# Sparse attention on one core: output projection in one stage, two groups' scores in the other bank ring, last query behind the scores

## What is computed

```python
proj = h @ w_in
q = rope_2(proj[..., :N_HEADS * HEAD_DIM] ...)
...
sc = einsum('bghqd,bgcd->bghqc', qb, kc) * scale        # compressed scores
p_c = masked_softmax(sc, ...);  o_c = p_c @ vc
p_s = masked_softmax(qb @ ks_g * scale, mask_s);  o_s = p_s @ vs_g
p_w = masked_softmax(qb @ kw * scale, mask_w);    o_w = p_w @ vw
out = gb[..., 0:1] * o_c + gb[..., 1:2] * o_s + gb[..., 2:3] * o_w
...
return o @ w_out
```

## Time and profile before

| | |
|---|---|
| runs of the kernel before | 1603.38, 1600.79, 1595.78 us; median 1600.79 |
| the profiled execution | 1603.51 us, of which the span of the trace is 1601.7 |
| TensorE busy | 1500.8 us, 94% of the span |
| VectorE, ScalarE busy | 1053.1 us (66%), 874.3 us (55%) |
| chain that ended last | 79% TensorE, 9% VectorE, 6% ScalarE, 3% transfers |
| mean granted clock of TensorE | 0.972 |

### The profile page before, as it was taken

How to read it: one execution, slowest core, us unless ns; L and a number is a source line. 1 busy time by engine, 2 the same in 40 slices (tenths; PEclk the granted TensorE clock), 3 DMA queues, 4 the chain that set the end, 5 groups by cost and what they waited for, 6 DMA issues and landing times.

```text
span 1601.7 us, 25719 instructions
## 1 busy us (share of the span) xinstructions
PE 1500.8 (94%) x10589; PEld 1410.6 (88%) x10589; DVE 1053.1 (66%) x1626; ACT 874.3 (55%) x1541; POOL 88.7 (6%) x141
## 2 busy tenths in 40 slices
PE   6998999999989989999999899999999888899997
PEld 6998889999989888899999799987998777899876
DVE  5645559886766366698868678855566434688744
ACT  6465557564554646564645666644566333566544
POOL 9100000006000000000000100000000000000000
PEclk9999999999999999999999999999899798999998
DMA  7524366566646143665666455565343011565561
GB/s 220 160 73 138 106 197 183 163 185 171 216 134 171 46 137 109 207 185 168 184 195 210 141 183 184 171 190 165 106 124 118 14 40 54 171 184 184 172 197 66
DMA packets 214692, 241.14 MB, mean 151 GB/s; under 512 B 19240, under 2 KB 185282, under 8 KB 214576
## 3 DMA queue, kind: packets, MB, share of 16 engines
q1 hardware_dynamic: 208672, 228.66, 47.8%
q0 software_dynamic: 5904, 10.85, 2.5%
HBM read 238.42 MB, written 1.05 MB: 150 GB/s over the span
## 4 chain that ended last, share of the span: by engine, by line
PE 79%; DVE 9%; ACT 6%; DMA 3%; issue 2%; POOL 0%; DVEq 0%; POOLq 0%
PE bank L589 23%; PE bank L593 22%; PE bank L592 22%; DVE w_lo L1642 2%; PE bank L688 2%; PE bank L760 2%; ACT w_hi L1160 2%; PE bank L1062 1%; DMA raw<-in_ffn_up 1%; ACT S L1328 1%; DMA raw<-in_w_in 1%; PE bank L1048 1%; PE bank L964 1%; DMA raw<-in_mla_w_ukv 1%; PE bank L788 1%
## 5 line engine op out<-in xcount | busy, mean ns | idle before, releaser
L1642 DVE TENSOR_TENSOR w_lo<-raw,w_hi 128x1024 fp32r<-128x1024 f32 (+2 forms) x460 | 523.8, 1154 | 296.2 <-ACT w_hi L1160 293.9
L589 PE MATMUL bank<-h_hi,w_hi 128*128 128x256 f32 (+1 forms) x2024 | 577.7, 285 | 21.1 <-DVE w_lo L1642 5.9
L1160 ACT CAST w_hi<-raw 128x1024 fp32r<-128x1024 f32 (+2 forms) x460 | 453.5, 991 | 244.7 <-DMA raw<-in_w_in 89.8
L592 PE MATMUL bank<-h_lo,w_hi 128*128 128x256 f32 (+1 forms) x2024 | 575.4, 284 | 0.0
L593 PE MATMUL bank<-h_hi,w_lo 128*128 128x256 f32 (+1 forms) x2024 | 575.3, 284 | 0.0
L589 PEld LDWEIGHTS bank<-h_hi,w_hi 128*128 128x128 f32 (+1 forms) x2024 | 390.1, 193 | 23.2 <-issue 17.9
L593 PEld LDWEIGHTS bank<-h_hi,w_lo 128*128 128x128 f32 (+1 forms) x2024 | 390.0, 193 | 0.0
L592 PEld LDWEIGHTS bank<-h_lo,w_hi 128*128 128x128 f32 (+1 forms) x2024 | 389.9, 193 | 0.1
L589 PE MATMUL bank<-w_hi,h_hi 128*128 128x512 f32 (+1 forms) x272 | 104.6, 384 | 12.9 <-DVEq L2386 10.2
L592 PE MATMUL bank<-w_lo,h_hi 128*128 128x512 f32 (+1 forms) x272 | 102.9, 378 | 0.0
L593 PE MATMUL bank<-w_hi,h_lo 128*128 128x512 f32 (+1 forms) x272 | 102.7, 378 | 0.0
(11 more groups left out here) (353 smaller groups left out, 2396.5 us busy)
## 6 DMA issues: line engine op xcount, KB each, us to landing
raw<-in_w_in SPq DMA_DIRECT2D x160, 512.0 KB, 3.8
raw<-in_ffn_up SPq DMA_DIRECT2D x88, 512.0 KB, 3.6
raw<-in_ffn_down SPq DMA_DIRECT2D x40, 512.0 KB, 4.4
raw<-in_w_proj_a SPq DMA_DIRECT2D x16, 512.0 KB, 3.4
raw<-in_w_proj_b SPq DMA_DIRECT2D x16, 512.0 KB, 3.4
raw<-in_w_out SPq DMA_DIRECT2D x16, 512.0 KB, 4.6
raw<-in_ple_gate SPq DMA_DIRECT2D x16, 512.0 KB, 3.8
raw<-in_w_proj_c SPq DMA_DIRECT2D x16, 384.0 KB, 3.3
```

The source lines that it names most:

```text
L589: first = pe.matmul(out_, lh, rh, start=start, stop=False)
L592: pe.matmul(out_, lh, rl, start=False, stop=False)
L1160: act.copy(w_hi[b][:, 0:size], raw[b][:, 0:size]).then_inc(sems["hi_done"], 1)
L1642: dve.tensor_tensor(w_lo[b][:, 0:size], raw[b][:, 0:size], w_hi[b][:, 0:size].bitcast(F32), ALU.subtract).then_inc(sems["w_split"], 1)
```

## The change

Four things, all of them a matter of order and of banks; the instructions and their sizes stay.

- The projection is one stage: project 0, C3, then projects 1, 2 and 3.
- With the J banks no longer held open, the scores of groups 2 and 3 and C1 take J banks (`LATE_SCORES`, thirteen J jobs, after which each engine advances J by 13). `score_job`, `scored`, `score_ring` choose the ring.
- Query 3 comes behind S1, and swap 3 behind X0. The new order of TensorE: S0, swap 2, S1, q3, X0, swap 3, V0, cs, S2, ct0, ct1, X1, V1, C0, S3, C1, X2, V2, X3, C2, V3, project 0, C3, project 1, 2, 3.
- ScalarE and VectorE follow: the splits of `w_out`'s first four pieces stand behind X0 on ScalarE and behind the three first operations on `Tc` on VectorE; ScalarE loads its exponential table with a small extra activation into `sink`; of X's banks VectorE copies 0, 1 and 4, ScalarE 2, 3 and 5.

```diff
@@ -181,12 +181,14 @@
 NSA_JOBS = (["bias"] + [f"norm{u}" for u in range(KT // 2)] + ["hidden", "keys0", "keys1", "kc", "vc", "gates", "kc_swap", "swap0", "swap1"]
-            + [f"S0.{i}" for i in range(6)] + ["swap2"] + [f"S1.{i}" for i in range(6)] + ["swap3", "cs"]
-            + [f"X0.{i}" for i in range(6)] + ["V0.1", "V0.0"] + [f"S2.{i}" for i in range(6)] + ["ct0", "ct1", "C0"]
-            + [f"X1.{i}" for i in range(6)] + ["V1.1", "V1.0"] + [f"S3.{i}" for i in range(6)] + ["C1"]
-            + [f"X2.{i}" for i in range(6)] + ["V2.1", "V2.0", "C2"]
-            + [f"X3.{i}" for i in range(6)] + ["V3.1", "V3.0", "C3"])
+            + [f"S0.{i}" for i in range(6)] + ["swap2"] + [f"S1.{i}" for i in range(6)]
+            + [f"X0.{i}" for i in range(6)] + ["swap3", "V0.1", "V0.0", "cs", "ct0", "ct1"]
+            + [f"X1.{i}" for i in range(6)] + ["V1.1", "V1.0", "C0"]
+            + [f"X2.{i}" for i in range(6)] + ["V2.1", "V2.0"] + [f"X3.{i}" for i in range(6)]
+            + ["C2", "V3.1", "V3.0", "C3"])
 NSA_AT = {name: n for n, name in enumerate(NSA_JOBS)}
+LATE_SCORES = {f"S{g}.{i}": 6 * (g - 2) + i for g in (2, 3) for i in range(6)}
+LATE_SCORES["C1"] = 12
 KV_ORDER = (0, 1, 2, 4, 3, 5)
@@ -952,8 +954,26 @@
 
+            def score_job(name):
+
+                if name not in LATE_SCORES:
+                    return job(name)
+                b = w.bank("J", LATE_SCORES[name])
+                pe.wait_ge(free[b], w.turn("J", LATE_SCORES[name]))
+                return b
+
+            def scored(name, mm, b):
+
+                mm.then_inc(sems[f"full{b}"], 1)
+                if name not in LATE_SCORES:
+                    w.go("K", 1)
+
             def emptied(name):
 
+                if name in LATE_SCORES:
+                    b = w.bank("J", LATE_SCORES[name])
+                    pe.wait_ge(free[b], w.turn("J", LATE_SCORES[name]) + 1)
+                    return
                 n = k0 + NSA_AT[name]
@@ -1016,19 +1036,20 @@
                 for n in range(4):
-                    b = job(f"S{g}.{n}")
+                    b = score_job(f"S{g}.{n}")
                     pe.matmul(ps[b][:, :], q2[:, 2 * g + n // 2, P:TOK],
                               kz[:, n % 2, g, :, :].rearrange("p a k -> p (a k)"), start=True, stop=False)
-                    filled(pe.matmul(ps[b][:, :].rearrange("p (a k) -> p a k", a=2)[:, :, P:TOK], ident_r[:, :],
-                                     causal_r[:, :].unsqueeze(1).to_broadcast([P, 2, P]), start=False, stop=True), b)
+                    scored(f"S{g}.{n}", pe.matmul(
+                        ps[b][:, :].rearrange("p (a k) -> p a k", a=2)[:, :, P:TOK], ident_r[:, :],
+                        causal_r[:, :].unsqueeze(1).to_broadcast([P, 2, P]), start=False, stop=True), b)
                 for u in range(2):
-                    b = job(f"S{g}.{4 + u}")
+                    b = score_job(f"S{g}.{4 + u}")
                     pe.matmul(ps[b][:, :].rearrange("p (a k) -> p a k", a=4), ident_r[:, :],
...
                                        q2[:, 2 * g + u, 0:P], kz[:, n, g, :, 0:P], start=False, stop=n == 1)
-                    filled(mm, b)
+                    scored(f"S{g}.{4 + u}", mm, b)
 
@@ -1064,7 +1085,7 @@
 
-                b = job(f"C{g}")
+                b = score_job(f"C{g}")
                 pe.wait_ge(sems["o_ready"], 2 * g + 2)
@@ -1072,19 +1093,18 @@
                                        om[:, g % 2, qt, u * P:(u + 1) * P], c["ident"], start=False, stop=qt == 1)
-                filled(mm, b)
+                scored(f"C{g}", mm, b)
 
...
 
-                if g == 0:
-                    for bank in range(4):
-                        pe.wait_ge(free[w.bank("J", bank)], w.turn("J", bank))
                 pe.wait_ge(sems["o_split"], g + 1)
...
                         bank = w.bank("J", u)
+                        if k == 0:
+                            pe.wait_ge(free[bank], w.turn("J", u))
                         cols = slice(n * 512, (n + 1) * 512)
@@ -1107,10 +1127,12 @@
             scores2(0)
-            query(3)
             swap(2)
             scores2(1)
+            query(3)
+            turn2(0)
             swap(3)
+            values2(0)
             b = job("cs")
@@ -1121,27 +1143,28 @@
             w.go("S", 4), w.go("J", 8)
-            turn2(0)
-            values2(0)
             scores2(2)
...
                                               for g in (2 * i, 2 * i + 1) for qt in range(TT)])
+            turn2(1)
+            values2(1)
             emptied("vc")
...
             combine2(0)
-            project2(0)
-            turn2(1)
-            values2(1)
             scores2(3)
             combine2(1)
-            project2(1)
-            for g in (2, 3):
-                turn2(g)
-                values2(g)
-                combine2(g)
+            turn2(2)
+            values2(2)
+            turn2(3)
+            combine2(2)
+            values2(3)
+            w.go("J", 13)
+            project2(0)
+            combine2(3)
+            for g in (1, 2, 3):
                 project2(g)
@@ -1570,15 +1593,20 @@
 
+            def score_ring(name):
+
+                return ("J", LATE_SCORES[name]) if name in LATE_SCORES else ("K", at(name))
+
             def query(i):
                 for n in range(2):
-                    hi(i, n)
+                    if i < 2:
+                        hi(i, n)
                     evac("J", 2 * i + n, q2[:, 2 * i + n, :], scale=SCALE2)
...
                 for i in range(6):
-                    b = w.bank("K", at(f"S{g}.{i}"))
+                    b = w.bank(*score_ring(f"S{g}.{i}"))
                     act.wait_ge(sems["t_max"], w.taken("t_max"))
@@ -1586,42 +1614,46 @@
                         ins_ = act.activation(dst, src, ACT.Exp, bias=nm[:, r, e:e + 1], accum_out=sums[:, r, e:e + 1])
-                    ins_.then_inc(free[w.bank("K", at(f"S{g}.{i}"))], 1)
+                    ins_.then_inc(free[b], 1)
 
             def turned2(g):
-                for n in (1, 3):
+                for n in (2, 3):
                     evac("K", at(f"X{g}.{n}"), t1T[:, n, :, :].rearrange("p b n -> p (b n)"), width=512)
...
             def high_o(g):
-                b = w.bank("K", at(f"C{g}"))
-                act.wait_ge(full[b], w.turn("K", at(f"C{g}")))
+                ring = score_ring(f"C{g}")
+                b = w.bank(*ring)
+                act.wait_ge(full[b], w.turn(*ring))
                 act.copy(h_hi[:, 2 * g:2 * g + 2, :].rearrange("p a n -> p (a n)"), ps[b][:, :])\
...
                 query(i)
+            act.activation(sink[:, :], c["eps"], ACT.Exp)
             exps2(0)
+            exps2(1)
             query(3)
-            exps2(1)
+            turned2(0)
+            for j in (2, 3):
+                hi(j, 0), hi(j, 1)
             act.wait_ge(sems["tc_ready"], 1)
...
             w.go("S", 4), w.go("J", 8)
-            turned2(0)
             exps2(2)
...
                 evac("K", at(f"ct{i}"), tcT[:, 2 * i:2 * i + 2, :].rearrange("p a n -> p (a n)"), width=512)
+            turned2(1)
             high_o(0)
-            turned2(1)
             exps2(3)
-            hi(0, 0), hi(0, 1)
             high_o(1)
             turned2(2)
-            hi(1, 0), hi(1, 1)
+            turned2(3)
             high_o(2)
-            turned2(3)
-            hi(2, 0), hi(2, 1)
+            w.go("J", 13)
+            hi(0, 0), hi(0, 1)
             high_o(3)
-            hi(3, 0), hi(3, 1)
+            for j in (1, 2, 3):
+                hi(j, 0), hi(j, 1)
             for u, (n, t) in enumerate(QUARTERS):
@@ -2328,12 +2360,17 @@
 
-            def maxima(g):
+            def score_ring(name):
+
+                return ("J", LATE_SCORES[name]) if name in LATE_SCORES else ("K", at(name))
+
+            def maxima(g, which=range(6)):
 
                 r = g % 2
-                for i in range(6):
-                    b = w.bank("K", at(f"S{g}.{i}"))
-                    dve.wait_ge(full[b], w.turn("K", at(f"S{g}.{i}")))
+                for i in which:
+                    ring = score_ring(f"S{g}.{i}")
+                    b = w.bank(*ring)
+                    dve.wait_ge(full[b], w.turn(*ring))
                     if i < 4:
@@ -2344,7 +2381,8 @@
                 for i in range(6):
-                    dve.wait_ge(free[w.bank("K", at(f"S{g}.{i}"))], w.turn("K", at(f"S{g}.{i}")) + 1)
+                    ring = score_ring(f"S{g}.{i}")
+                    dve.wait_ge(free[w.bank(*ring)], w.turn(*ring) + 1)
                 settle(dve.reciprocal(rg[:, r, :], sums[:, r, :]))
@@ -2352,7 +2390,7 @@
 
-                for n in (0, 2, 4):
+                for n in (0, 1, 4):
                     b = w.bank("K", at(f"X{g}.{n}"))
@@ -2376,13 +2414,14 @@
 
-                b = w.bank("K", at(f"C{g}"))
-                dve.wait_ge(full[b], w.turn("K", at(f"C{g}")))
+                ring = score_ring(f"C{g}")
+                b = w.bank(*ring)
```

(34 more changed lines are left out.)

## The result

The changed kernel took **1580.1 us** (median of 4 runs, 1577.4 to 1585.8) against 1599.9 for the kernel before (4 runs): ratio 0.988, 95% interval 0.985 to 0.991. The forecast was 1579, from 1570 to 1591. Over all of them the changed kernel's median is 1582.5 (30 runs, 1572.4 to 1592.6) and that of the kernel before 1596.9 (45 runs, 1587.2 to 1606.4). The gain over many runs is therefore 14.4 us, less than the 21.5 that the sum took off the profiled execution. Why is the subject of the next sections.

The account below looks back on a forecast made before the run. TensorE bounds the attention stretch by work, gaps and half-speed time: 1226.5 + 92.6 work + 9.9 gaps + 3 low clock + 1.9 idle puts ple at 1333.9, 21.5 us earlier; from the 1600.8 median, 1579 us (1570 to 1591).

Parts of the forecast that it names:

- the sum: Total of all terms: the ple product behind the projection starts at 1333.9 instead of 1355.4, 21.5 us earlier.
- First scores: End of S0: 1.2 us earlier, as a weight split leaves VectorE's queue before the second rotation; bounds 0 and 1.3.
- The way to cs: From S0's end to cs's end: work, with cs at 3.5 us and swaps at 1.0, plus 0.8 of bank waits in S1.
- The first gap: In S2: S2.4 waits 4.6 us for exponentials, delayed by VectorE's Tc operations and four weight splits, until 8.5 after cs.
- the clock step: Low clock behind the second gap, in X1 and V1, costs 3 us, bounds 0 and 7; behind the first, largely hidden.
- The second gap: In X1: X1.2 waits 4.0 us, until 17.0 after cs, for ScalarE to empty ct0's bank behind S2's exponentials.
- V1 to the end: From V1 on nothing waits long: no wait over 0.7 us to V3's end; the low_o and om waits go.
- The clock rival: Clock stays low from X1 to V3, 35 us of work taking twice as long: 1611 us, chance 0.07 for the full case.
- Transfers and late VectorE: Two rivals: projection paced by its transfers, 1585 to 1587, chance 0.1; VectorE late at nine steps, 1585, chance 0.1.
- The tail: After the projection TensorE idles 1.9 us, where it idled 0.4, before the ple product; behind that nothing differs.

Follow-up runs that it names:

- the second experiment: Changed kernel with ScalarE copying ct0, ct1 and its part of X1 after the first two of S2's six banks of exponentials: 1573.5 us against 1583.4.
- e10: The changed kernel with nothing altered, run a fourth time: 1580.9 us.
- e7: The changed kernel with nothing altered, run again on the chip of the second group of experiments: 1582.1 us.
- e1: Changed kernel with VectorE's four weight splits moved ahead of its wait for the compressed scores: 1576.9 us against 1583.4.
- e5: Changed kernel with the last query put back ahead of swap 2 and of S1's exponentials on ScalarE: 1580.4 us against 1582.1.
- e8: Changed kernel with LATE_SCORES emptied (one bank ring) and the last query back ahead of swap 2: 1581.0 us against 1580.9.

## Why the prediction was right, and where it was not

**First scores.** Forecast −1.2; swap 2 now starts 6.3 us after S0's start where the query did at 7.4: 1.1. Right.

**The way to cs.** Forecast 26.15 us from the end of S0 to the end of cs. TensorE starts S2 at 1254.01, 32.3 after S0's start at 1221.74, of which S0 is 6.3: 26.0. The bank waits in S1 that I put at 0.8 were 0.2 and a swap 0.9 for 1.0, but cs took 4.0 and not 3.5, half of its time at clock 0.50: three small misses that cancel.

**The first gap.** The place and the time of its end are right, its size is not. The sum had S2.4 start 8.5 us after cs; it started at 1262.62, 8.6 after. But TensorE waited there 1.6 us and not 4.6, because it ran the four banks before it at clock 0.51 (1253 to 1260 in the first view). So the term of the wait was 3.0 too high, and the same 3.0 went into low clock at no cost to the end. Filling a wait with half-speed work is what "largely hidden" in the clock step meant, but it named no clock that falls ahead of the gap: nothing waited there, and the clock fell inside cs in every trace of the changed kernel.

**The second gap.** Forecast: S2.5 free at 10.6 after cs, `tc_done` at 11.1, X1.2 at 17.0, a wait of 4.0. Measured: ct runs from 1265.05 (11.0), X1.2 at 1270.89 (16.9), wait 3.9. Right, and for the reason given, as the second experiment showed by moving only ScalarE's order.

**The clock: the term that was mis-sized.** Forecast 3 us behind the second gap, bounds 0 and 7. In the first trace X1's rest took 3.5 for 1.8, V1 10.1 for 5.4 and C0 3.2 for 1.9: 7.7 us, just over the upper bound. The rows I had (a low stretch of 9 us) gave no such length, and no single row could have: four traces of one kernel gave 17 us of it twice (7.7 and 7.6 us lost), once about 3 us (1.5 lost, e10) and once none behind that wait (e7). The mean loss is 4.2. That the forecast of 3 is near it is luck: I scaled one execution's loss. The whole stretch shows the same. The prediction makes it 113.6 us (1333.9 less S0's start in before, 1220.33); the mean of the four is 113.8, and none of them is within 2.9 of it.

**The same in before.** This is the step that misjudged the gain. I took 15.4 us of low clock out of a single execution of before and let 12.4 of it go. The second trace of before has 8.8 (129.24 less 1.27 for ple, 98.9 + 1.1 for the slower first scores, and 19.2 of waits behind them). The profiled execution, 1603.5, stands 6.6 above the median of 45 runs. The stretch of the changed kernel was summed from work and gaps upward, but the time was had by taking the difference of 21.5 from runs of before, and that was too large by 7.1: the three runs that it was taken from have a median 3.9 above the one of 45 (1600.8), and the changed kernel came out 3.2 above the unrounded 1579.3 over its 30 runs. In the first four runs it was 0.8 above. So the closeness of the first result is in part luck.

**V1 to the end.** Forecast: no wait over 0.7 from V1 to the end of V3. There is none. The six waits for `low_o` and `om` are gone because the splits of three groups are done before the projection begins and the last one runs under quarter 1: the earlier trace rows against the waits of the changed kernel, and 23.50 us busy of 23.50 in the projection. The load of o2b and its cast stay covered.

**The clock rival fell.** X2, V2, X3, C2 and V3 are 18.7 us without a dense product, and the clock was 1.00 throughout (fourth row of the first view), as in the 8 us that the prediction weighed. The 48 transposes of X2 and X3 stand there between 96 narrow value products, so this does not test transposes alone. The rule of the Trainium skill (TensorE: Matmul & The Clock Gate, section "Part 4: PE-mode transpose") that transposes do not count as busy may hold for a stretch of nothing else, which no run here has. What it was used for, that this mixture would bring the clock down, did not happen in any of the traces.

**Transfers and late VectorE.** Neither rival came: no wait for `w_lo`, and no moved gap.

**The tail.** Forecast: ple idles 1.9 and nothing differs behind. It idled 1.4. From the ple product to the end the four traces of the changed kernel took 241.1, 246.6, 243.8 and 245.1 us, the two of before 246.3 and 243.0: means of 244.1 and 244.6. "Nothing differs" holds over several executions. In the first pair of traces alone it looks wrong by 5.2 us, which happened to cancel the 4.7 of the clock term.

**What stays open.** The mean stretch fell by 18.3 us (132.1 to 113.8), the medians by 14.4. Of the rest, 2.2 us lie ahead of S0, which starts at 1223.3 on average in the four traces and at 1221.1 in the two of before, with TensorE's order the same there. Two traces of before are too few to say more. What decides between an execution with and one without the 17 us at low clock was not found, nor whether it is settled ahead of the wait for `tcT`, where the traces already differ.

## What to carry to other kernels

Take from a trace the moment at which a wait ends (S2.4 and X1.2 repeated to 0.5 us in four traces) but not the wait's length, which shrank by up to 1.5 us when the work ahead of it ran slowly; and price the low clock from more than one execution: it moved one unchanged kernel's stretch by 7.5 us. Before a chain of waits is cured by a second set of banks, look at what the banks wait for: here both rings stood behind the same exponentials, the ring was worth about 1 us in the traces and nothing in the medians, and reordering ScalarE's copies 3.6 in the traces. A stage gathered at the end pays when its inputs are finished early by engines that idle: the four waits for them, 10.2 us, went and nothing took their place. And when several parts change together, undoing two of them doesn't give the whole gain to the third: 5 to 8 us came from ahead of S2.

## What the runs showed of the hardware

- The granted clock fell without a gap. In the four traces of the changed kernel it went from 1.00 to 0.50 (2.4 to 1.2 GHz) 30.9 to 31.4 us after S0's start, inside cs (32 columns a matmul, 28.3 to 32.3 us after it in the first trace), with no wait of TensorE since S1 and TensorE busy 7.00 of 7.00 us behind the fall.
- Once low, narrow work may not lift it. In two traces X1's rest, V1 and C0 ran 16 of 17 us busy at 0.50 before it rose. In the two others V1 ran at 1.00. When high, the same kinds of work kept it at 1.00 for 18.7 us.
- The length of a wait does not settle it. One of 3.0 us (e1) left the clock up, and waits of 1.3 us in before had it at 0.50 behind them. One of 3.9 stood ahead of each long low stretch. In e5 and e8, with the query ahead of S1, the clock stayed up through cs and the first banks of S2 and fell at the 4.4 us wait behind them, for about 7 us (0.51 from 1263 to 1270 in e5).
